# Hybrid layers of a four-layer kernel: the eight local-attention head pairs moved from the attention stage into the convolution panels, and the gated delta rule in three steps a slot instead of two

## What is computed

```
h = rms_norm(x) * (1 + scale) + shift ;  parts = split(h @ w_in)
o_a = banded_attention(rope(aq), rope(ak), av, window=128, sinks)      # 4 heads, 2 kv heads
o_b = nsa_mixer(bq, ...)   # 4 heads, each: compressed keys + selected keys + window of 512, gated
q,k,v = silu(causal_conv4(cqkv)) ; q,k = l2norm(q), l2norm(k)
o_c = gated_delta_rule(q, k, v, a, b)     # 4 heads of 128, chunks of 64: triangular solve, then a scan
o_c = rms_norm(o_c) * silu(z)
x = x + gate * (concat(o_a, o_b, o_c) @ w_out) ;  x = x + gate_f * mlp(rms_norm(x))
```

## Time and profile before

| | |
|---|---|
| median of 3 runs | 2777.2 us |
| the profiled execution | 2780.78 us |
| its span, first to last instruction | 2779.3 us |
| mean granted TensorE clock | 0.993 |
| convolution stage of the first hybrid layer | 1356.6 to 1463.5 us |
| attention stage of the first hybrid layer | 1463.5 to 1616.7 us |
| slots 0 to 23 of it | 1463.5 to 1573.4 us |
| slots 0 to 23 in the second hybrid layer | 2201.7 to 2310.7 us |

### The profile page before, as it was taken

The page is one execution under the profiler, slowest core; times in us unless marked ns, Lnnn a source line. Parts: engine busy times, 40 slices in busy tenths (PEclk is TensorE's granted clock), DMA queues, the critical chain, the costliest instruction groups (busy, mean ns, idle before and its releaser), DMA issues.

```text
span 2779.3 us, 41753 instructions
## 1 busy us (share of the span) xinstructions
PE 2674.1 (96%) x17218; PEld 2114.3 (76%) x17218; DVE 1625.2 (58%) x2919; ACT 1159.3 (42%) x2016; POOL 9.4 (0%) x21
## 2 busy tenths in 40 slices
PE   7999999999999999999998899999999988999998
PEld 6777888867666788886886667888878766788886
DVE  7887556654556864667556755444565577533334
ACT  3754324235555432424546543222354466322222
POOL 0000000000000000000000000000000000000000
PEclk9999999999999999999999999999999999999999
DMA  8364555532221465553330024344433200222232
GB/s 311 114 220 144 189 173 177 181 127 77 77 71 60 138 203 189 196 182 116 99 130 2 3 69 137 132 150 143 147 128 103 81 3 2 99 98 96 95 98 83
DMA packets 92092, 336.40 MB, mean 121 GB/s; under 512 B 10480, under 2 KB 10736, under 8 KB 91776
## 3 DMA queue, kind: packets, MB, share of 16 engines
q1 hardware_dynamic: 86656, 314.87, 34.4%
q10 hardware_dynamic: 3936, 14.64, 1.5%
q0 software_dynamic: 1312, 4.23, 0.5%
HBM read 331.57 MB, written 2.13 MB: 120 GB/s over the span
## 4 chain that ended last, share of the span: by engine, by line
PE 46%; ACT 4%; DVE 4%; issue 1%; DVEq 0%; ACTq 0%
PE bank L664 12%; PE bank L666 12%; PE bank L665 12%; ACT probs L2313 1%; PE bank L942 1%; PE bank L927 1%; PE bank L913 1%; PE bank L1014 1%; PE bank L707 0%; PE bank L709 0%; PE bank L708 0%; PE bank L1108 0%; PE bank L1176 0%; PE bank L1002 0%; DVE probs L1642 0%
## 5 line engine op out<-in xcount | busy, mean ns | idle before, releaser
L1278 DVE TENSOR_TENSOR weights_low<-weight_ring,weights_high 128x1024 fp32r<-128x1024 f32 x404 | 493.6, 1223 | 414.9 <-ACT weights_high L2046 414.6
L664 PE MATMUL bank<-in_high,weights_high 128*128 128x512 f32 x1800 | 707.6, 393 | 7.3 <-DVE in_low L1427 3.1
L666 PE MATMUL bank<-in_high,weights_low 128*128 128x512 f32 x1800 | 702.0, 390 | 0.0
L665 PE MATMUL bank<-in_low,weights_high 128*128 128x512 f32 x1800 | 701.8, 390 | 0.0
L2046 ACT ACTIVATE weights_high<-weight_ring 128x1024 fp32r<-128x1024 f32 x404 | 424.6, 1052 | 407.5 <-PE bank L666 302.3
L664 PEld LDWEIGHTS bank<-in_high,weights_high 128*128 128x128 f32 x1800 | 338.7, 188 | 83.8 <-DVE in_low L1427 5.0
L666 PEld LDWEIGHTS bank<-in_high,weights_low 128*128 128x128 f32 x1800 | 338.6, 188 | 71.3
L665 PEld LDWEIGHTS bank<-in_low,weights_high 128*128 128x128 f32 x1800 | 338.6, 188 | 69.9 <-issue 0.7
L664 PE MATMUL bank<-hidden_split,weights_high 128*128 128x512 f32 x896 | 349.5, 390 | 0.2 <-ACT hidden L2060 0.2
L665 PE MATMUL bank<-hidden_split,weights_high 128*128 128x512 f32 x896 | 348.6, 389 | 0.0
L666 PE MATMUL bank<-hidden_split,weights_low 128*128 128x512 f32 x896 | 348.6, 389 | 0.0
(11 more groups left out here) (395 smaller groups left out, 3353.0 us busy)
## 6 DMA issues: line engine op xcount, KB each, us to landing
weight_ring<-stream SPq DMA_DIRECT2D x596, 512.0 KB, 3.4
mixer_out<-cmp ACTq DMA_DIRECT2D x6, 1024.0 KB, 4.9
hidden<-forget_rows POOLq DMA_DIRECT2D x16, 256.0 KB, 3.6
residual<-x ACTq DMA_DIRECT2D x4, 512.0 KB, 8.0
mixer_out<-cmp SPq DMA_DIRECT2D x2, 1024.0 KB, 6.2
out<-mixer_out ACTq DMA_DIRECT2D x4, 512.0 KB, 2.7
constants<-consts ACTq DMA_DIRECT2D x1, 1821.5 KB, 9.7
silu_c<-c ACTq DMA_DIRECT2D x2, 512.0 KB, 4.4
```

The costliest lines, as they stand in the source:

```text
L664: pe.matmul(bank[:, :], WHI[:, z, cols], high, start=(k == 0), stop=False)
L665: pe.matmul(bank[:, :], WHI[:, z, cols], low, start=False, stop=False)
L666: ins = pe.matmul(bank[:, :], WLO[:, z, cols], high, start=False, stop=(k == ktiles - 1))
L1278: v.tensor_tensor(WLO[:, z, :], ring[:, n % RING, :], WHI[:, z, :].bitcast(F32), ALU.subtract).then_inc(*mark("weights_low", "low", n))
```

## The change

It changes the two hybrid layers alone; the instructions of the first two layers and their order stay as they are.

- The slot's parts become functions (`attention(name, items, where)` gives scores, product, turn on PE; maxima, normalise, turned on DVE; exps, turned, scaled on ACT), with the places of scores, probabilities and transposes in a tuple `Places`.
- The 8 local pairs leave the slot loop and are written out between the panels of the convolution stage, as ("swa", l). Their scores lie in banks 4 and 6, their two transposes in halves of banks 2 and 3, the probabilities in `mixer_out` tiles. The two results are copied to the tiles of the rotated queries (`hyb_in`), which are free by then.
- ACT keeps its Exp table through these pairs: `z(0)` and `z(1)` are evicted with Copy, all Silu of the stage (`conv_out`, `z_silu`, `hidden`) come in one run behind the last Exp. The swaps of keys come earlier; `next_weights` issues the compression's DMAs apart from `hidden`.
- `decays` moves from behind `z(0)` to behind `compress(1, 0)`; `cmp2` from before `z(3)` to behind it.
- 24 pairs in 26 slots. The 46 steps of the solve stand one in slot 0, three in each of slots 1 to 15; the scan's 16 steps two in each of slots 16 to 23. A third part, fill(d, 2), stands behind the second transpose.
- The filler before the first rows step goes.

```diff
-    HYB_ENDS = {3: 0, 7: 1, 19: 2, 31: 3}
+    HYB_ENDS = {11: 2, 23: 3}
+    SWA_AT = Places(whole(B[4], B[6]),
+                    [M[:, a, 256 * z:256 * z + 256] for a in (AK, KSW) for z in range(2)],
+                    [B[2][:, 256:512], B[3][:, 256:512]], [PT[:, z, 256:512] for z in range(2)])
-    HYB_SLOTS, FOX_SLOTS = 34, 34
-    STEPS = {(1 + n // 2, n % 2): what for n, what in enumerate(delta_steps())}
+    HYB_SLOTS, FOX_SLOTS = 26, 34
+    places = [(0, 2)] + [(d, n) for d in range(1, 16) for n in range(3)] + [(d, n) for d in range(16, 24) for n in range(2)]
+    STEPS = dict(zip(places, delta_steps()))
...
             conv(0)
+            pe.wait_ge(*at("tok_out", l, NTB - 1))
+            pe.wait_ge(*at("swapped", l, "ak"))
+            scores(0)
             conv(1)
+            pe.wait_ge(*at("swapped", l, "ks"))
+            scores(1)
             z(0)
+            turns(0)
+            scores(2)
+            conv(2)
+            product(0)
+            turns(1)
+            scores(3)
+            conv(3)
+            product(1)
+            turns(2)
+            scores(4)
+            conv(4)
...
             compress(1, 1)
-            conv(11)
+            z(3)
             pe.wait_ge(*at("cmp2_landed", l))
...
             ins.then_inc(*mark("tensor_hybrid", "cmp2", l))
-            z(3)
             attention_and_delta(l)
...
             if name == "rows":
                 h, = which
-                if h == 0:
-                    busy(B[5], 3)
...
+            z(0, ACT.Copy)
+            turned(0)
+            exps(2)
+            prepare(ahead(("conv", l, 2)))
+            scaled(2)
+            conv_in(2, 0)
+            turned(1)
...
+            conv_out(0)
+            conv_out(1)
+            conv_out(2)
+            z(2)
```

More of the change, by code:

```diff
@@ L905, in paired_attention @@
+        def paired_attention(name, items, where, slots, begin, fill, out_free):
+            n, (scores, product, turn) = len(items) // 2, attention(name, items, where)
             for d in range(slots):
@@ L907, in paired_attention @@
                     begin(d)
[L908 to L917, removed]
+                    scores(d)
                 fill(d, 0)
@@ L1632, in paired_attention @@
+        def paired_attention(name, items, where, slots, bias, fill, end):
+            n, (maxima, normalise, turned) = len(items) // 2, attention(name, items, where, bias)
             for d in range(slots):
-                c = 8 * (d % 4)
                 if d < n:
-                    for z in range(2):
-                        i = 2 * d + z
-                        it, w = items[i], items[i]["width"]
-                        bias(i)
-                        v.wait_ge(*at(*name, "scores", i))
-                        if i >= 4:
-                            v.wait_ge(*at(*name, "turns", i - 4))
-                        v.tensor_tensor_reduce(probs[i % 4][:, 0:w], B[2 + z][:, 0:w], it["mask"], -1.0, it.get("least", 3.0e38),
-                                               ALU.add, ALU.min, COL[:, c + z:c + z + 1]).then_inc(*mark(sem, *name, "max", i))
+                    maxima(d)
@@ L2475, in hybrid @@
             s.activation(COL[:, 84:88], vec2(l, "A_log"), ACT.Exp).then_inc(*mark(sem, "a_exp", l))
+            exps, turned, scaled = attention(("swa", l), swa_items(l), SWA_AT)
             conv_in(0, None)
+            swap(KSW, KS2, KW2, "ks")
+            exps(0)
+            prepare(ahead(("conv", l, 1)))
+            scaled(0)
             conv_in(1, None)
+            exps(1)
+            prepare(ahead(("z", l, 0)))
+            scaled(1)
+            z(0, ACT.Copy)
+            turned(0)
@@ new lines, in hybrid @@
+            exps(2)
+            prepare(ahead(("conv", l, 2)))
+            scaled(2)
+            conv_in(2, 0)
+            turned(1)
+            exps(3)
+            prepare(ahead(("conv", l, 3)))
+            scaled(3)
+            conv_in(3, 1)
+            turned(2)
+            exps(4)
+            prepare(ahead(("conv", l, 4)))
+            scaled(4)
+            conv_in(4, 2)
+            turned(3)
+            exps(5)
+            prepare(ahead(("z", l, 1)))
+            scaled(5)
+            z(1, ACT.Copy)
```

427 lines of the change are left out of this document (274 added, 153 removed).

## The result

| | before | after |
|---|---|---|
| median of the runs, us | 2776.3 (4 runs, 2771.2 to 2777.9) | 2791.7 (4 runs, 2789.8 to 2793.1) |
| ratio to before, 95% interval | | 1.0055 (1.0042 to 1.0068) |
| profiled execution, us / span / mean granted clock | 2780.8 / 2779.3 / 0.993 | 2789.8 / 2788.3 / 0.990 |

The change makes the kernel slower by 15.3 us, just over the top of my range and on the wrong side of "no change". The two profiled executions are only 9.0 us apart: that of before lies 4.4 us above its median, that of after 1.9 under its own. The first of these is part of the answer.

What follows compares the result with a forecast made beforehand. It took PE, busy 96% of the span, as the bound. Convolution stage +14.5 us and attention stage -13.9 gave +0.6 a layer, +1.2 for two: 2782 in profile terms, 2778 us against the median, range 2762 to 2791.

Steps and rivals of the forecast that it cites:

- my term of 14.5: Convolution stage: the eight local pairs add 14.0 us of PE work and panel starts 0.5, +14.5 us a layer.
- rival four: Convolution stage: DVE or ACT come late, 1 us at each of 8 places, two layers, +16 us, 2794; chance 0.06.
- Entry: Attention stage, last convolution panel to first rows step: 5.3 us, against 4.5 plus 0.7 of cmp2 before.
- levels 2 to 4: Levels of the solve in the attention slots: one slot each, 4.8 us from p to p, against 5.8 before.
- the last piece: Attention stage, end of the second four levels to old slot 24, now 16: 8.0 us, against 8.4 before.
- the model of a slot set by DVE's loop: Level slots: DVE's loop from first maximum to transposed copy sets the slot, 4.8 us, against PE work of 3.6 to 4.2.
- rival two: Attention slots: levels stay at 5.8 us, slots 0 to 15 take 104 us, two layers lose 16, 2794; chance 0.13.
- third head's rows to its first p: Attention stage, from the third head's rows step to the second first p: 18.0 us, against 19.8 before.
- I count as many such falls after as before: Clock: falls like the profile's 3.4 us one, costing PE 1.7 us, stay equal in number, so they add nothing.
- The transfer from profile to median: Whole kernel: the profiled 2780.8 us lies 3.6 above the median, so 2782 in its terms became 2778.
- Rival three: Clock: small matmuls closer together bring three more falls a layer of 1.7 us each, +10 us, 2788; chance 0.07.
- Rival one: Attention slots: waits shrink with the slots, which take 88 us; a layer gains 7.2 us, two 14, 2764; chance 0.30.

Runs made afterwards that it cites:

- e3: After with fillers in every long wait of PE in attention slots 0 to 10; 2784.2 us, ratio to before 1.0025.
- e1: After with the three filler matmuls put back at the entry, ahead of the first head's rows; 2785.4 us, ratio to before 1.0033.
- e9: e10 with fillers added in the other long waits; 2775.2 us, ratio to before 0.9996.
- e10: e7 with 32 decays matmuls ahead of the last panel and 32 behind it in the entry's wait, with two fillers; 2779.5 us, ratio to before 1.0008.
- e7: e1 with the second compression's last product and cmp2 ahead of the last panel, and the 64 decays matmuls split in two runs; 2780.6 us, ratio to before 1.0015.
- e12: e1 with the second compression's last product and cmp2 ahead of the last panel, the 64 decays matmuls left in one run; 2784.6 us, ratio to before 1.0032.
- e4: The weaving alone: after with the 62 delta steps two a slot again in 34 slots; 2802.4 us, ratio to before 1.0090.
- e5: The packing alone: before with the delta steps three a slot, local pairs still in the slots; 2825.2 us, ratio to before 1.0177.
- e11: Before with its decays split around the last panel as in e10, 32 of them replacing two of three entry fillers; 2776.0 us, ratio to before 0.9997.
- e6: e1 with DVE's level 1 mask earlier and ACT's copy of the second pair's X ahead of its scaling; 2786.6 us, ratio to before 1.0044.

## Why the prediction was wrong

- **The convolution stage**: I forecast 106.9 to 121.4 us; it is 117.8 and 120.9. Both of before's stages hold a fall of 3.4 us that costs 1.7; after's second one holds 6.8 that cost 3.4, its first none. Without them 105.2 goes to 117.8 and 117.5, +12.5 us, or +13.2 for the local pairs, as cmp2 with its 0.7 has left the stage: my term of 14.5 was 1.3 us too high. (The mark of 121.4 forgets those 0.7, which the entry's 5.3 already has; it should read 120.7.) PE has no gap, so rival four did not happen.
- **Entry** 5.1 us (5.3 forecast), levels 2 to 4 at 4.7 to 5.0 (4.8), 8.6 us to the third head's rows (8.5), the last piece 6.8 (8.0), the eight levels without falls 40.3 (19.4 and 20.95 in e3, 39.5 forecast). This fits the model of a slot set by DVE's loop, and rivals one and two are refuted: the stage's 102.5 us alone could pass for rival two's 104, but the levels without a fall stand 4.7 to 5.0 us apart (first pair of heads). One piece was mis-sized: third head's rows to its first p, 18.0 forecast, 19.25 measured and 20.0 with fillers in it.
- **What luck there was**: without falls a layer would come to some 0.4 us over the forecast (1.3 less in the convolution stage, 1.75 more in the slots, by e3). Two misses of opposite sign hide each other there.
- **The step that failed** is the sentence "I count as many such falls after as before". In the profiled execution each layer has three falls of 6.8 us in slots 0 to 15 (behind the entry, at both first p steps), where the old slots 0 to 23 had three in both layers together (6.8, 3.4 and 3.4 us). Over both hybrid layers it is 47.8 us in place of 27.3, as before also has a fall of 3.4 us behind the norms of each layer, which after has not. Over all runs PE spent 56 us low in place of 29. By before's own runs (mean 2772.0 us at clock 0.997, 11 runs; 2779.6 at 0.993, 18 runs) 22 us low cost 7.6, 0.34 us each; where PE bounds, up to 0.5 (3.1 us for a fall of 6.8, by after's two convolution stages). The 26.5 us more come to 9 to 13 of the 15.3 us, an estimate. Shown by experiments: 6.3 us by the entry's fillers (e1), 4.2 by the others (e9 against e10), 4 by the decays (e7 against e12), each on a different form of the kernel, so they are not to be added. Fillers give back less than the price: e3's 7.4 us for 30 us less at 1.2 GHz are 0.25 each.
- **The transfer from profile to median** failed with it. I took before's profiled execution as 3.6 us slow and shifted the sum by that. It stood at 0.993, as only 19 of before's 83 runs do or lower, so it held more falls than most; after's four runs all stood at 0.990. An offset made of falls is no constant that a changed kernel keeps. In terms of the profiled pair the forecast of +1.2 missed by 7.8 us, in terms of the medians by 13.7: the step from one to the other nearly doubled the miss.
- **Rival three** was the right mechanism, with 2788 for a measured 2791.7, and I gave it 0.07. It blamed the small matmuls closer together; e4 has them no closer in steps a slot and falls as often, so taking the local pairs out is enough (0.90 and 0.91), as packing is (e5). The rule of the Trainium skill ("TensorE: Matmul & The Clock Gate", Part 1), that little activity halves the clock and sustained work brings it back, had named the entry, and the trace agrees there: PE waits 3.24 us, and the clock is 0.50 behind it. I set it aside on the means 0.95 and 0.98: they showed that falls were rare with the old spacing, not with the new. But the rule alone doesn't say which filler pays: the same three matmuls are worth 6.3 us in after and nothing in before.
- **Slips in the working**, none of which changes the outcome: the clock did fall in the dense panels too (0.98 in before's convolution stage), so "not in the dense panels around it" is wrong. The second four levels of before took 6.2 us each, not 5.8 (24.7 / 4). Rival one's 14 us come off the forecast of 2778, though they are a gain on 2777.2: 2763. And levels of 4.6 to 5.1 us alone give 2775 to 2783, not 2771 to 2785.
- **What stays open**: why the falls in after are 6.8 us long and those of before often 3.4, and why before's bare entry, with its falls, costs nothing over all runs. The runs show where the clock fell and what stood before it, not more. Also, e9's edits beyond the fillers would help before less (e11), so "level with before" is not a like for like comparison: with the best found for each, after's form is 3 us behind (2775.2 against 2772.1; their intervals, 0.9988 to 1.0005 and 0.9973 to 0.9991, overlap by a hair).

## What to carry to other kernels

A change that takes large matmuls out from between small ones, or packs small ones closer, should be priced with the granted clock as a term of its own: list each long wait followed by a chain of small matmuls, and each run of matmuls of few columns next to another, and put a bound on a fall there. Fillers belong in waits that are there anyway, placed last, when the order stands, and each measured. Where an edit leaves the median as it was, look in the trace whether its wait shrank and a fall took the gain (e6). And read the clock of every run before taking one profile's distance to the median as a constant.

## What the runs showed of the hardware that I had not expected

PE busy 16.00 of 16.00 us and the granted clock still at 0.79 (e12): the fall needs no idle time, it came as 64 matmuls of 31 columns gave way to 64 of two. The same binary's runs spread over 10 us (2770.8 to 2781.8 for before), and most of that goes with the recorded clock: 0.997 and 2772, 0.993 and 2780. And a slot stretch can be at full clock with 15 us of waits in it (e9, 2209.8 to 2308.5, PE busy 83.76 of 98.70 us, clock 1.00), so the share of busy time doesn't tell where the clock falls.
